# Pieces of the first attention's maxima moved into the last blocks of the projection ahead of it

## The reference

```python
def dense_block_attention(q, k, v):
    ...
    def one(qblk):
        s = jnp.einsum("bqhgd,bkhd->bhgqk", qblk, k).astype(jnp.float32) * scale
        p = jax.nn.softmax(s, axis=-1).astype(v.dtype)
        return jnp.einsum("bhgqk,bkhd->bqhgd", p, v)

def even_mixer(hx, hc, w_in, w_out, gk_w, gk_b, gla_g, qn_g, kn_g, cos, sin, with_ctx):
    ...
    aqx, akx = apply_rope(aqx, cos, sin), apply_rope(akx, cos, sin)
    k_all = jnp.concatenate([akx, akc], axis=1)
    v_all = jnp.concatenate([avx, avc], axis=1)
    ax = dense_block_attention(aqx, k_all, v_all)
    ox = jnp.concatenate([gla_out(oxf + flip(oxb), gx), ax], axis=-1) @ w_out
    ...
    ac = dense_block_attention(aqc, akc, avc)
    oc = jnp.concatenate([gla_out(ocf + flip(ocb), gc), ac], axis=-1) @ w_out
```

## Time and profile before

| | |
|---|---|
| median of 3 runs | 1670.89 us (1669.6 to 1671.86) |
| profiled execution | 1669.06 us, of which the span of the profile is 1667.3 us |
| TensorE matmuls busy | 1577.1 us (95%) |
| VectorE busy | 896.4 us (54%) |
| ScalarE busy | 553.3 us (33%) |
| GpSimd busy | 592.8 us (36%) |
| granted clock of TensorE, mean | 0.976 of 2.4 GHz |

### The profile page before, as it was taken

How to read it: one execution, slowest core, us unless ns; L and a number is a source line. 1 busy time by engine, 2 the same in 40 slices (tenths; PEclk the granted TensorE clock), 3 DMA queues, 4 the chain that set the end, 5 groups by cost and what they waited for, 6 DMA issues and landing times.

```text
span 1667.3 us, 25157 instructions
## 1 busy us (share of the span) xinstructions
PE 1577.1 (95%) x10716; PEld 1309.2 (79%) x10716; DVE 896.4 (54%) x1253; ACT 553.3 (33%) x720; POOL 592.8 (36%) x263
## 2 busy tenths in 40 slices
PE   6898968867999999999999999999999999999997
PEld 3787854446888888888888888865568998998995
DVE  5688575655947776656556633556734221221224
ACT  4743434425332211222122234335444321232232
POOL 1263234521323332332222223235554444444442
PEclk9999988979999999999999999999999999999998
DMA  8433110004323333333443311210003223223222
GB/s 331 179 114 114 40 39 1 1 3 162 129 77 126 127 127 126 127 127 127 132 141 120 110 67 64 77 39 1 1 30 96 90 89 97 93 89 107 97 89 101
DMA packets 41631, 158.61 MB, mean 95 GB/s; under 512 B 4624, under 2 KB 5008, under 8 KB 39728
## 3 DMA queue, kind: packets, MB, share of 16 engines
q1 hardware_dynamic: 41232, 156.74, 27.2%
q0 software_dynamic: 288, 0.26, 0.1%
HBM read 154.89 MB, written 2.10 MB: 94 GB/s over the span
## 4 chain that ended last, share of the span: by engine, by line
PE 79%; DVE 9%; issue 5%; ACT 3%; POOL 2%; DMA 1%; SPq 0%; DVEq 0%; POOLq 0%; ACTq 0%
PE psum L1645 65%; PE psum L1818 3%; DVE mx L1165 2%; PE psum L1723 1%; PE psum L1788 1%; DVE product L1035 1%; POOL acc L581 1%; PE psum L1665 1%; PE psum L1833 1%; DMA ada_w<-ada_dram 1%; PE psum L1805 1%; PE psum L1790 1%; DVE big L1083 1%; PE psum L1792 1%; PE psum L1794 1%
## 5 line engine op out<-in xcount | busy, mean ns | idle before, releaser
L1645 PE MATMUL psum<-act,whi 128*128 128x512 f32 (+1 forms) x4064 | 807.4, 319 | 3.1 <-DVE act L1466 2.5
L607 POOL TENSOR_TENSOR wlo<-raw,whi 128x1024 fp32r<-128x1024 f32 (+1 forms) x181 | 445.3, 2460 | 937.4 <-ACT whi L638 937.4
L1645 PEld LDWEIGHTS psum<-act,whi 128*128 128x128 f32 x4064 | 604.9, 189 | 63.6 <-issue 4.8
L1645 PE MATMUL psum<-act,wlo 128*128 128x512 f32 (+1 forms) x2032 | 485.2, 317 | 0.0
L1035 DVE SCALAR_TENSOR_TENSOR product<-adr,cb 128x1024 f32<-128x1024 f32 x128 | 280.7, 2225 | 139.6 <-DMA adr<-adat_dram 129.0
L1645 PEld LDWEIGHTS psum<-act,wlo 128*128 128x128 f32 x2032 | 317.1, 190 | 27.9
L638 ACT ACTIVATE whi<-raw 128x1024 fp32r<-128x1024 f32 (+1 forms) x181 | 188.0, 1039 | 317.9 <-DMA raw<-weights_dram 317.6
L1083 DVE SCALAR_TENSOR_TENSOR tmps<-psum,rs 128x256 f32<-128x256 f32 (+1 forms) x176 | 78.1, 485 | 200.3 <-PE psum L1645 195.5
L1645 PE MATMUL psum<-gh,whi 128*128 128x512 f32 (+1 forms) x528 | 160.9, 358 | 0.0
L1645 PE MATMUL psum<-gh,wlo 128*128 128x512 f32 (+1 forms) x528 | 160.8, 359 | 0.0
L1645 PE MATMUL psum<-gl,whi 128*128 128x512 f32 (+1 forms) x528 | 159.4, 355 | 0.0
(11 more groups left out here) (179 smaller groups left out, 1233.0 us busy)
## 6 DMA issues: line engine op xcount, KB each, us to landing
raw<-weights_dram SPq DMA_DIRECT2D x181, 512.0 KB, 3.5
adr<-adat_dram SPq DMA_DIRECT2D x80, 512.0 KB, 4.5
ada_w<-ada_dram SPq DMA_DIRECT2D x8, 1024.0 KB, 15.1
xT<-x_in_dram SPq DMA_DIRECT2D x4, 1536.0 KB, 12.9
cb<-crow_dram SPq DMA_DIRECT2D x2, 1024.0 KB, 8.1
out_dram<-big SPq DMA_DIRECT2D x8, 256.0 KB, 2.2
con<-consts_dram SPq DMA_DIRECT2D x1, 512.0 KB, 7.4
con<-consts_dram SPq DMA_DIRECT2D x1, 320.0 KB, 3.6
```

Source lines behind the costliest of these rows:

```text
L607: nc.gpsimd.tensor_tensor(wlo[:, s, 0:w], raw[:, s, 0:w], whi[:, s, 0:w].bitcast(F32), ALU.subtract).then_inc(sem("s_lo"), 1)
L1645: last = MM(out_[:, o:o + t1 - t0], w_, a_[:, t0:t1], start=k == order[0] and j == 0, stop=k == order[-1] and j == 2)
```

## The change

Unit 0's only piece and the six of unit 1 are done inside the projection: (0,0) behind block 15, (1,0) in the middle of block 16, (1,1) to (1,3) in and behind block 17, (1,4) and (1,5) in block 18. The product `rows` of unit 0 is behind block 17. They use banks 4-7, as the blocks hold banks 0-3. ScalarE's `q_high` of tiles 0 to 3 go behind blocks 14, 15, 17 and 18, `minus_top(0, 0)` ahead of the bias of block 18. VectorE's reductions are put among its work, `carry(0)` and the low part of query tile 0 go to block 15, `carry(2)` to block 16, `normed(3)` and `normed(4)` behind the reductions of their block, and `given(1)` and the low part of tile 1 behind the projection. GpSimd's copies of the decays (`keep_of`) are issued a block earlier. `beside(n)` stands ahead of the late modulation products for all n. The fence is gone: TensorE waits instead for the scaling of block 17 before the first scores, and for the last reduction (`mx` 7) before the second.

```diff
-def pieces_first(layer):
-    return [(0, 0)], [(1, p) for p in range(4)]
+def pieces_within(m, k):
+    return {(15, 8): (0, 0), (16, 4): (1, 0), (17, 3): (1, 1), (17, 6): (1, 2), (17, 8): (1, 3), (18, 3): (1, 4),
+            (18, 6): (1, 5)}.get((m, k))
...
-    if layer == 0 and i == 0 and a == 0:
-        return [(1, 4)], [(1, 5)]
...
-        negm = [at(f"negm{L}", [P, 2, NX], O_OSB[L] + 8 * NX, F32R) for L in range(2)]
+        negm = [at(f"negm{L}", [P, 2, NX], (O_PROD, O_OSB[1] + 8 * NX)[L], F32R) for L in range(2)]
...
+            if L == 0 and i < 2:
+                return (6, 7) if p == 0 else (4, 5)
...
-            return bank(6 if L == 1 and i == 0 else 0)
+            return bank((7, 6)[L] if i == 0 else 0)
...
-                if n == 17:
+                if n == 16:
                     pool.wait_ge(sem("g_pos"), 3)
...
+                if n == 14:
+                    act.wait_ge(sem("s_atd"), late_sums(N_LATE0))
+                    q_high(0, 0)
...
                     head_square(4)
+                    q_high(0, 1)
                 if n == 16:
                     head_root(4)
+                if n in (17, 18):
+                    q_high(0, n - 15)
...
-                    fence(act, 1)
                     attention(0)
...
+                if n == 18:
+                    act.wait_ge(sem("g_carry"), 2)
+                    minus_top(0, 0)
...
                 if L == 0:
-                    q_low(0, 0)
-                    taken(0, pieces_first(0)[0])
                     q_low(0, 1)
-                    taken(0, pieces_first(0)[1])
+                    given(1)
...
                 if n == 16:
-                    carry(0)
+                    taken(0, [(0, 0)])
                     carry(1)
+                    carry(2)
                 if n == 17:
-                    carry(2)
                     carry(3)
                     given(0)
                 if n == 18:
-                    given(1)
+                    taken(0, [(1, 3)])
...
+                if n == 15:
+                    q_low(0, 0)
+                    carry(0)
+                if n == 16:
+                    taken(0, [(1, 0)])
+                    normed(3)
+                if n == 17:
+                    taken(0, [(1, 1), (1, 2)])
+                    normed(4)
+                if n == 18:
+                    taken(0, [(1, 4), (1, 5)])
...
+                if kind == "proj" and L == 0:
+                    beside(n)
                 for i in late_tiles(n):
                     late_modulation(i)
-                if kind == "proj" and L == 0:
-                    beside(n)
...
-                    if kind == "proj" and L == 0 and k == 4:
+                    if kind == "proj" and L == 0 and k == (3 if n == 17 else 4):
                         within_block(n)
+                    if kind == "proj" and L == 0 and pieces_within(n, k):
+                        maxima(0, *pieces_within(n, k))
...
+                    if t == 1:
+                        pe.wait_ge(*(na("mx", 0, 7) if L == 0 else na("rsin", 1, 9)))
...
+                    pe.wait_ge(*ev(FIRST[("out", 0)] - 2))
...
                     means(3)
+                    pe.wait_ge(sem("a_rsin"), 3)
                 if n == 16:
                     pe.wait_ge(sem("a_rs"), 4)
                     rotated(0, 3)
-                    pe.wait_ge(sem("a_rsin"), 3)
+                    pe.wait_ge(*na("mx", 0, 2))
                     means(4)
                 if n == 17:
                     pe.wait_ge(sem("a_rs"), 5)
+                    pe.wait_ge(sem("s_idr"), 32)
+                    rows(0, 0)
                     rotated(0, 4)
+                if pieces_within(n, 8):
+                    maxima(0, *pieces_within(n, 8))
```

More of the change, by code:

```diff
@@ L343, in build @@
                  "s_gh", "s_gl", "s_fin", "s_outdma",
-                 "s_fence", "s_nln", "a_ln", "g_nln"] + [f"s_raw{i}" for i in range(RING)]
+                 "s_nln", "a_ln", "g_nln"] + [f"s_raw{i}" for i in range(RING)]
         names += [f"s_{n}" for n in ("sq", "sqadd", "nps", "rs", "nhh", "nhl")]
@@ L485, in edges_of @@
             return cols[:, a:a2 + 1:a2 - a, :], band[:, b:b2 + 1:b2 - b, :]
-        def fence(eng, k):
-            eng.drain().then_inc(sem("s_fence"), 1)
-            eng.wait_ge(sem("s_fence"), 3 * k)
         block = ctx.enter_context(nc.Block())
@@ L890, in out_high @@
                     A(mix_tile(L, u)[0], osb[L][:, i % 2, 0:u["nq"]], ACT.Copy).then_inc(sem("a_ohi"), 1)
[L892 to L897, removed]
                 for i, u in enumerate(units):
@@ L1419, in heads_inputs @@
                     roped(0, 2)
[L1420 to L1426, removed]
+                if n in (17, 18):
+                    roped(0, n - 14)
             def gla():
@@ L1485, in _ @@
                     mod_scale(1)
-                    fence(dve, 1)
                     attention(0)
@@ L1711, in maxima @@
                     pe.wait_ge(*na("qhi", L, u["j"] + 1))
-                if L == 1 and m == 0:
-                    pe.wait_ge(*na("khi", 1, 1))
-                    pe.wait_ge(*na("vtok", 1, 1))
+                if m == 0:
+                    pe.wait_ge(*na("khi", L, 1))
+                    pe.wait_ge(*na("vtok", L, 1))
                 if piece_banks(L, i, p)[0] == 0 and i >= 1:
@@ L1779, in scores @@
                         pe.wait_ge(*na("exp", L, t - 1))
-                    if L == 1 and t == 1:
-                        pe.wait_ge(*na("rsin", 1, 9))
+                    if t == 1:
+                        pe.wait_ge(*(na("mx", 0, 7) if L == 0 else na("rsin", 1, 9)))
                     keys, qs = slice(kt * P, kt * P + P), slice(q0 + qa, q0 + qb)
@@ L1979, in within_block @@
                     updates(2)
+                if n == 17:
+                    pe.wait_ge(sem("a_rsin"), 4)
             def gla():
@@ L2055, in _ @@
                 if n == FIRST[("out", 0)]:
-                    fence(pe, 1)
                     attention(0)
```

## The result

The changed kernel takes 1651.72 us (median of four executions, 1651.53 to 1651.86) against 1671.38 us (four, 1669.6 to 1673.06), a ratio of 0.9882 with a 95% interval of 0.9865 to 0.99: 19.7 us less, where 14.8 were forecast. It lies just under the low end of the stated range (1652.0). The direction and the place were forecast. The size was not, and two waits that were forecast inside the blocks did not appear. The two profiled spans differ by 17.5 us (1667.3 to 1649.8).

A forecast was written before the change was run, and what follows sets the result against it. TensorE was taken as the bound, with a 26.6 us seam between block 18 and unit 1 holding little matmul. The terms start unit 1 at 242.0 against 256.84, 14.8 us off 1670.89: 1656.1 us, range 1652 to 1661.

The forecast's parts named there:

- Keys ahead: Before block 13: key copies ahead of late modulation give TensorE a lead of 2.1 us, bounds 1.8 and 3.7.
- step 6: Start of unit 1: clock taken as falling in the seam's idling, gain 0; 1.5 us if it stays up.
- rival B: Clock stays up over the seam's gap, or VectorE is not held by GpSimd: gain 16.3 to 19 us; 20%.
- Pieces: Blocks 15 to 18: seven pieces at 0.4 us each cost TensorE 2.8 us, unit 0's row product another 0.4.
- The first new wait: Rotation behind block 16 waits for query tile 3's normalisation on VectorE: 2.3 us, bounds 0 and 3.5.
- The second new wait: Block 17: piece (1,2) waits for the reduction of (1,1): 0.9 us, bounds 0 and 3.3.
- Block 18 and the seam: Block 18 ends at 234.6, 4.3 us later; unit 1 starts 7.4 us after that, at 242.0 against 256.84.
- The clock at the seam: Between block 18 and unit 1: TensorE idles 2.3 to 3.2 us and the clock falls, as before; gain 0.
- C: VectorE's queue becomes the bound, GpSimd delaying block 17's product of the states by 2.4 us: gain 7 to 12.5; 16%.
- D: Not faster: seven pieces wait on late VectorE reductions, 2.6 us per piece, 18 us together; time 1671 or more; 3%.
- step 3: Rotation behind block 16: wait of 2.3 us if GpSimd and VectorE exclude each other in SBUF, 1.2 without.

The follow-up runs named there:

- changed_again: The changed kernel, unchanged under a second name, with more executions on another day's chip: 1650.62 us, ratio 0.9884.
- gpsimd_over_scans: The changed kernel with four more unused GpSimd products of 128x512 at the time of VectorE's two scans in block 16: 1655.34 us, ratio 0.9909.

## Why the prediction was wrong in size

1. **Keys ahead.** The wait went from 3.70 to 1.57 us by ScalarE's copy, as forecast. At the end of block 15 the lead is 1.9 us, against 2.1 forecast. What I had wrong is the clock: step 6 and rival B used the 3.70 us gap as a case in which it does not fall. It falls there in two of three profiles and costs up to 2.3 us more. The part is worth 3.3 us alone, by medians. This is about 1.2 us of the miss.
2. **Pieces.** The term was 0.4 us each, and it is 0.6: around the piece at 213.24 the spacing of the block's groups is 1.57 and 1.16 us against 1.05. From the mean product behind block 15 to the end of block 18, seven pieces and a row product cost 4.7 us (34.5 from 196.81 in place of 29.8 from 200.46) where I had 3.2. Above my value, within my bounds of 0.24 to 0.8.
3. **The first new wait.** This is the step that failed. It took 5.55 us for two scans and 2.3 us of waiting for TensorE. The scans take 3.40, and the subtraction comes after the normalisation has begun; the wait is 0. I had divided a merged pair that had a GpSimd operation inside it, and so counted the exclusion twice: in the scans and again as blocking.
4. **The second new wait.** 0.9 was taken, 0 was measured, by the same scans.
5. **Block 18 and the seam.** Counted from block 2, block 18 ends 2.8 us later than before (231.27 - 48.55 against 230.27 - 50.33), not 4.3: the 3.2 us of waits missing, 1.5 more for pieces and 0.2 less lead. From there to unit 1 it takes 7.95 us, not 7.4, because the clock has fallen before the values, which take 1.05 and not 0.6.
6. **The clock at the seam.** It fell, as taken. The gap was 3.9 us, above my 2.3 to 3.2, since the scores of 256 columns take 0.6 us a step and not up to 1.3.

The terms side by side, in us gained, counted from block 2:

| term | forecast | measured |
|---|---|---|
| lead from the keys | 2.1 | 1.9 |
| seven pieces and a row product | -3.2 | -4.7 |
| the two new waits | -3.2 | 0 |
| the seam, from block 18 to unit 1 | 19.2 | 18.6 |
| sum | 14.8 | 15.8 |

So the term that was off by most is the waits, 3.2 us, and the other errors happen to take two thirds of it back. That the sum of the rows comes within 1.0 us is luck. The other 3.9 us of the miss lie outside the terms of the sum. Part is the clock in the gap before block 13. Part comes from stretches whose code the change leaves alone. Block 2 starts at 50.0 to 50.3 in the three profiles without the pieces moved and at 48.0 to 49.9 in the ten with them, 1.2 us earlier on average. From unit 1 to the end it is 1411.1 us on average in the three and 1409.3 in the ten, though with a spread of 4 us. No run tests why, so this part of the cause stays open.

Of the rivals, B was right in half: VectorE was not held by GpSimd, and the clock did fall. C did not happen, but both experiments that lengthen a queue show that it was close: a wait of 3.3 to 3.8 us appears when either engine gets four small operations more. The gain of 19 to 20 us is above the range of B too. For D seven late pieces would have been needed, and none was late.

The rule weighed in step 3 (the Trainium skill, SBUF — State Buffer, "Who interferes with whom") holds better than I said. I wrote that the scans agreed only in part; they fit it once a scan is taken at 1.75 us: the subtraction issued inside the first scan ends at 210.98, 2.3 us after that scan, and the second scan 1.6 us after the subtraction.

## What to carry to other kernels

Ask of a fence what is queued behind it. Here the rows show no cost of the fence itself. The serial row of small products behind it, each waiting for a reduction on another engine, made up most of a seam of 26.6 us, which is 7.95 us without it; inside blocks of dense products each costs 0.6 us. Before pricing an operation from a merged row, ask for it alone: a duration may contain another engine's turn. And after an edit, look for what the chain still does that its first consumer does not need; here that was worth another 5 to 6 us.

## What the runs showed of the hardware that I had not expected

The same idle gap of 3.70 us on TensorE left the granted clock at 1.00 in one execution and brought it to a mean of 0.57 over the next five microseconds in another, in the same program (2.3 us). A wait of only 1.99 us after several microseconds of products at full clock brought it to half (changed_again, block 11), and one of 2.00 us did not (gpsimd_over_scans). A VectorE operation that waits for GpSimd shows the waiting inside its own duration: a scan of 1.75 us is recorded with 3.88, a 0.68 us product with 2.53. Two matmuls of 64 rows that are busy for 0.50 us move the stream around them by 0.63.
